# Down products of the two Conv FFN layers: from 24 plain weight tiles per layer to Strassen products over two 256-token halves, in three chunks

## The reference, cut to what matters

```python
def conv_ffn(x, w_up, conv_w, conv_b, w_down):
    u = causal_depthwise_conv(x @ w_up.astype(x.dtype), conv_w, conv_b)
    g, val = jnp.split(u, [FFN_DIM_2], axis=-1)
    return (jax.nn.gelu(g) * val) @ w_down.astype(x.dtype)

def second_block(...):
    ...
        h = h + conv_ffn(rms_norm_2(h, ffn_norm[layer]), ffn_w_up[layer], ffn_conv_w[layer],
                         ffn_conv_b[layer], ffn_w_down[layer])
```

## Time and profile before

| | |
|---|---|
| median of three runs | 2938.49 us |
| lowest, highest | 2938.44, 2938.96 us |
| span of the profiled execution, first to last instruction | 2937.1 us |
| TensorE busy | 2919.6 us, 99% |
| VectorE, ScalarE, GpSimd busy | 1309.0, 1288.6, 1322.3 us |
| up stage of the first layer | about 2000 to 2262 us of the span |
| down stage of the first layer | 2262.57 to 2393.1 us |
| down stage of the second layer | 2802.8 to 2933.5 us |

### The profile page before, as it was taken

The page is one execution under the profiler, slowest core; times in us unless marked ns, Lnnn a source line. Parts: engine busy times, 40 slices in busy tenths (PEclk is TensorE's granted clock), DMA queues, the critical chain, the costliest instruction groups (busy, mean ns, idle before and its releaser), DMA issues.

```text
span 2937.1 us, 40238 instructions
## 1 busy us (share of the span) xinstructions
PE 2919.6 (99%) x14312; PEld 2388.5 (81%) x14312; DVE 1309.0 (45%) x2190; ACT 1288.6 (44%) x2017; POOL 1322.3 (45%) x743
## 2 busy tenths in 40 slices
PE   9999999999999999999999999999999999999999
PEld 7888888888878888888888877778888887888887
DVE  5657534221063667434222076654554138455510
ACT  4556545322253556444223265554444228444421
POOL 4454355444434554455444443444444443444443
PEclk9999999999999999999999999999999999999999
DMA  4222232323322232333333322212333322233333
GB/s 145 73 87 80 81 122 92 99 94 100 108 86 87 73 98 68 94 115 106 94 99 101 108 80 71 61 56 94 98 95 98 95 94 94 93 100 93 100 104 90
DMA packets 77275, 273.37 MB, mean 93 GB/s; under 512 B 8776, under 2 KB 9416, under 8 KB 77152
## 3 DMA queue, kind: packets, MB, share of 16 engines
q1 hardware_dynamic: 74112, 266.05, 29.0%
q10 hardware_dynamic: 3040, 5.64, 0.6%
HBM read 269.55 MB, written 2.10 MB: 92 GB/s over the span
## 4 chain that ended last, share of the span: by engine, by line
PE 93%; DVE 2%; ACT 2%; POOL 1%; issue 1%; DMA 0%; SPq 0%; DVEq 0%; ACTq 0%; POOLq 0%
PE ps L822 25%; PE ps L824 25%; PE ps L823 25%; PE ps L1122 2%; PE ps L1153 2%; PE ps L1100 2%; PE ps L1375 2%; PE ps L1381 1%; PE ps L1376 1%; PE ps L1226 1%; PE ps L1232 1%; PE ps L1227 1%; ACT WHI L1534 1%; PE ps L1095 1%; PE ps L1097 0%
## 5 line engine op out<-in xcount | busy, mean ns | idle before, releaser
L2894 POOL TENSOR_TENSOR WLO<-WRAW,WHI 128x1024 fp32r<-128x1024 f32 x393 | 949.8, 2419 | 1158.5 <-ACT WHI L1534 1158.2
L822 PE MATMUL ps<-HH,WHI 128*128 128x512 f32 x2144 | 842.1, 393 | 2.4 <-POOL WLO L2894 0.9
L824 PE MATMUL ps<-HH,WLO 128*128 128x512 f32 x2144 | 834.8, 389 | 0.0
L823 PE MATMUL ps<-HL,WHI 128*128 128x512 f32 x2144 | 834.4, 389 | 0.0
L1534 ACT ACTIVATE WHI<-WRAW 128x1024 fp32r<-128x1024 f32 x467 | 490.6, 1051 | 281.6 <-DMA WRAW<-wall 280.8
L822 PEld LDWEIGHTS ps<-HH,WHI 128*128 128x128 f32 x2144 | 402.5, 188 | 91.2 <-issue 5.3
L824 PEld LDWEIGHTS ps<-HH,WLO 128*128 128x128 f32 x2144 | 402.4, 188 | 84.7
L823 PEld LDWEIGHTS ps<-HL,WHI 128*128 128x128 f32 x2144 | 402.7, 188 | 81.1
L2746 DVE SCALAR_TENSOR_TENSOR ps<-U,COLS,ps 128x512 f32<-128x512 f32 x192 | 145.0, 755 | 122.6 <-ACT ps L1993 108.5
L2228 DVE TENSOR_TENSOR ACC<-ACC,SQ 128x512 f32<-128x512 f32 x78 | 68.4, 877 | 280.5 <-ACT SQ L1819 271.1
L2980 POOL TENSOR_SCALAR SG<-SG,RS 128x512 f32<-128x512 f32 (+3 forms) x104 | 109.9, 1067 | 141.1 <-DVE RS L2508 141.1
(11 more groups left out here) (422 smaller groups left out, 4805.4 us busy)
## 6 DMA issues: line engine op xcount, KB each, us to landing
WRAW<-wall SPq DMA_DIRECT2D x502, 512.0 KB, 3.5
y<-X ACTq DMA_DIRECT2D x8, 256.0 KB, 4.0
X<-xin SPq DMA_DIRECT2D x3, 512.0 KB, 7.9
DFT<-dft ACTq DMA_DIRECT2D x4, 258.0 KB, 4.3
PT_IN<-pin ACTq DMA_DIRECT2D x2, 512.0 KB, 3.7
DIL<-dil ACTq DMA_DIRECT2D x1, 768.0 KB, 4.6
X<-xin SPq DMA_DIRECT2D x2, 256.0 KB, 4.7
COLS<-cols ACTq DMA_DIRECT2D x1, 290.5 KB, 5.3
```

Of the source, the lines that this page charges most:

```text
L822: pe.matmul(out_, WHI[w_at], x_hi, start=first, stop=False)
L823: pe.matmul(out_, WHI[w_at], x_lo, start=False, stop=False)
L824: return pe.matmul(out_, WLO[w_at], x_hi, start=False, stop=last)
L2894: pool.tensor_tensor(WLO[:, s, :], whole, WHI[:, s, :].bitcast(F32), ALU.subtract).then_inc(wt_lo, 1)
```

## The change

The down stage becomes three chunks. A chunk is 4 rounds of up (8 activation tiles), then a stage `down` that adds these 8 tiles' share to the output. There, output tiles go in pairs, activation tiles in pairs, and tokens in two halves of 256: a 2x2 by 2x2 block product, made by 7 block products instead of 8. Each is three matmuls of 256 columns. The first two chunks have 4 output pairs; the third has 3, and its last two output tiles are made plainly, with two units of 24 matmuls of 512 columns. There are 24 down units per layer as before.

The 7 products need sums. Of the weights: VectorE makes four sums of 128x256 for each paired unit (`sums_of`), one of them in place; ScalarE then splits 1024 and another 768 columns (`split_paired`), and GpSimd the same (`remainder_paired`). Of the activations: VectorE makes three more operations at the end of each up round (`mixed`), ScalarE one copy of 128x1024, VectorE one more remainder of 128x1024. Of the outputs: after each pair, ScalarE copies one half bank out and VectorE makes seven additions (`pair_added`). A pair uses banks 0 to 3 or 4 to 7 in turn. The pairs of a chunk are made one after another, and a pair waits for the additions of the pair two before it. The first pair of a chunk waits until VectorE has emptied all of banks 0 to 3. The loops of `conv_ffn` are written out.

```diff
+CHUNKS = ((0, 4), (4, 4), (8, 4))
...
+PRODUCTS = ((0, "slot", A11, B11), (2, "slot", A12, B21), (4, "slot", A22, T4), (6, "slot", A21, T3),
+            (5, "extra", S1, T1), (1, "extra", S2, T2), (3, "extra", S4, B22))
...
-        if gain:
-            residual("F2", FT2, gain)
+        for k0, m in CHUNKS:
...
+            add("down", 1, pairs * m // 2 + 2 * last, 8, per, made=up, heads=pairs, last=last, gain=gain)
...
+            def down(st):
+                up, blocks = st.made, blocks_of(st)
...
+                for j, (p, b) in enumerate(order_of(st)):
+                    if b == 0 and p == 0:
+                        for k in range(4):
+                            pe.wait_ge(bank_free[st.bank(k)], st.use(k))
+                    if b == 0 and p == 1:
+                        pe.wait_ge(S["product_ready"], up.at("product_ready", 2, up.reps - 1))
+                    if b == 0 and p >= 2:
+                        pe.wait_ge(S["pair_step"], st.at("pair_step", PAIR_STEPS * (p - 1)))
+                    weights(st.unit(j))
...
+                    for i in range(2):
+                        k = 2 * b + i
+                        if p == 0:
+                            pe.wait_ge(S["operand_ready"], up.at("operand_ready", 3, k))
+                        for h, home, block_, x in PRODUCTS:
...
+                            pe.matmul(o, w_hi, FTH[:, row, cols_], start=first, stop=False, skip_group_check=True)
+                            pe.matmul(o, w_hi, FTL[:, row, cols_], start=False, stop=False, skip_group_check=True)
+                            mm = pe.matmul(o, w_lo, FTH[:, row, cols_], start=False, stop=last, skip_group_check=True)
+                    mm.then_inc(unit_used, 1)
...
+            def split_paired(n):
+
+                s, q = n % SLOTS, PAIRED[n]
+                act.wait_ge(raw[s], 16 * (n // SLOTS + 1))
+                act.wait_ge(weights_summed, 4 * q + 2)
+                act.activation(WHI[:, s, :], WRAW[:, s, :], ACT.Copy).then_inc(slot_hi, 1)
+                act.wait_ge(weights_summed, 4 * q + 4)
+                act.activation(XHI[:, q % EXTRA, :], XRAW[:, q % EXTRA, :], ACT.Copy).then_inc(wt_hi, 1)
...
                     for j in range(4):
...
+                        sums_of(st, j, r)
                         dve.wait_ge(unit_used, st.unit(j, r) + 1)
                         scaled(st, j, r, U[:, j, 2:2 + SEQ])
...
+                            if j == 3:
+                                mixed(st, r, halves(SG), (2, 3, 6, 7))
+                            remainder(st, (FTH[:, 4 * r + j // 2, :], FTL[:, 4 * r + j // 2, :]), SG[:, j, :], 1 + j // 2, r)
+                    remainder(st, mixed_rows(r), TM[:, :, :], 3, r)
...
+            def sums_of(st, j, r=0):
...
+                dve.wait_ge(raw[s], 16 * (n // SLOTS + 1))
+                dve.tensor_tensor(sum_of(e, S1), at[A21], at[A22], ALU.add).then_inc(weights_summed, 1)
+                dve.tensor_tensor(at[A21], at[A21], at[A11], ALU.subtract).then_inc(weights_summed, 1)
+                dve.wait_ge(weights_summed, 4 * q + 2)
+                dve.tensor_tensor(sum_of(e, S2), at[A22], at[A21], ALU.add).then_inc(weights_summed, 1)
+                dve.wait_ge(weights_summed, 4 * q + 3)
+                dve.tensor_tensor(sum_of(e, S4), at[A12], sum_of(e, S2), ALU.subtract).then_inc(weights_summed, 1)
...
+            def pair_added(st, p):
...
+                dve.wait_ge(S["first_copied"], st.at("first_copied", p + 1))
+                step(dve.tensor_tensor(t[:, 3, :], t[:, 0, :], bank[0][:, HALF:SEQ], ALU.add))
+                step(dve.tensor_tensor(y1, y1, bank[1][:, :], ALU.add))
+                wait(1)
+                step(dve.tensor_tensor(t[:, 1, :], t[:, 3, :], bank[2][:, HALF:SEQ], ALU.add))
+                step(dve.tensor_tensor(t[:, 2, :], t[:, 3, :], bank[3][:, 0:HALF], ALU.add))
+                step(dve.tensor_tensor(y2, y2, bank[2][:, :], ALU.add))
+                wait(3)
+                step(dve.tensor_tensor(y1, y1, TM[:, 0, :], ALU.add))
+                wait(5)
...
+            def down(st):
+                for j in range(st.units):
+                    p = ended_at(st, j - 1)
+                    if p is not None:
+                        pair_added(st, p)
+                    sums_of(st, j)
...
+            def remainder_paired(n):
...
+                pool.wait_ge(weights_summed, 4 * q + 4)
+                pool.wait_ge(slot_hi, q + 1)
+                pool.tensor_tensor(WLO[:, s, :], WRAW[:, s, :], WHI[:, s, :].bitcast(F32), ALU.subtract)
+                pool.wait_ge(wt_hi, n + 1)
+                pool.tensor_tensor(XLO[:, e, :], XRAW[:, e, :], XHI[:, e, :].bitcast(F32), ALU.subtract).then_inc(wt_lo, 1)
```

More of the change, by code:

```diff
@@ L124, with pair_order @@
 COL, N_COLS = column_plan()
+def pair_order(pairs, blocks):
+    return [(p, b) for p in range(pairs) for b in range(blocks)]
 def unit_list():
@@ L164, in conv_ffn @@
     def conv_ffn(l):
[L165 to L169, removed]
+        for k0, m in CHUNKS:
+            last = 2 * (k0 + m) == FT2
+            for n in range(2 * k0, 2 * (k0 + m)):
+                product("ffn_w_up_2", l, DM, n * P)
+                product("ffn_w_up_2", l, DM, FFN2 + n * P)
+            for p, b in pair_order(DT // 2 - last, m // 2):
+                u.append(("ffn_w_down_2 paired", l, k0 + 2 * b, 2, 2 * p * P, 2 * P))
+            if last:
+                for n in range(DT - 2, DT):
+                    u.append(("ffn_w_down_2", l, 2 * k0 * P, 2 * m * P, n * P, P))
     for c in range(6):
@@ L195 @@
 FOLDS = {n: f for f, n in enumerate(FOLD_UNITS)}
+PAIRED = {n: q for q, n in enumerate(n for n, unit in enumerate(UNITS) if unit[0].endswith(" paired"))}
 HOSTS = ("fourier_branch", "branch_mla")
@@ L540, in build @@
         unit_used = sem("unit_used")
+        weights_summed, slot_hi = sem("weights_summed"), sem("slot_hi")
         bank_free = [sem(f"bank_free{b}") for b in range(BANKS)]
@@ new lines, in down_tail @@
+            def down_tail(st, j0):
+                pe.wait_ge(S["pair_step"], st.at("pair_step", 2 * PAIR_STEPS))
+                for n in range(2):
+                    weights(st.unit(j0 + n))
+                    s, kt = st.unit(j0 + n) % SLOTS, 2 * st.made.reps
+                    for i in range(kt):
+                        row = 4 * (i // 2) + i % 2
+                        mm = three(ps[4 + n][:, :], (slice(None), s, slice(i * P, i * P + P)), FTH[:, row, :], FTL[:, row, :], i == 0, i == kt - 1)
+                    mm.then_inc(unit_used, 1)
@@ new lines, in down @@
+            def down(st):
+                for j in range(st.units):
+                    p = ended_at(st, j - 1)
+                    if p is not None:
+                        pair_added(st, p)
+                    sums_of(st, j)
+                    if st.last and j == st.units - 1:
+                        tail_added(st, DT - 2, j - 1)
+                    p = ended_at(st, j - 2)
+                    if st.last and p is not None:
+                        for t in range(2):
+                            finished(st, 2 * p + t)
+                if st.last:
+                    finished(st, DT - 2)
+                    tail_added(st, DT - 1, st.units - 1)
+                    finished(st, DT - 1)
+                else:
+                    pair_added(st, st.heads - 1)
@@ L2923, in units @@
                 last = st.u0 + st.reps * st.units + AHEAD >= NU
-                repeat(pool, st, body, st.reps if last or st.put_off else 1)
+                repeat(pool, st, body, st.reps if last or st.put_off or st.kind in ("conv_ffn", "down") else 1)
             def operand(st):
```

152 lines of the change are left out of this document (135 added, 17 removed).

## The result

The kernel with the change takes 3026.25 us (median; 3024.66 to 3028.63), the kernel before 2938.47 (2938.44 to 2938.96): 1.0298 times as long, 95% interval 1.0283 to 1.0313. The forecast was 3042 with a range of 2957 to 3085, slower at 0.91. On the span the change costs 3023.6 - 2937.1 = 86.5 us where the sum said 103.4.

What follows compares the result with a forecast made beforehand. TensorE, busy 99% of 2937.1 us, was taken as the bound. Waits of 121.8 us less 18.4 saved gave +103.4, so 3040.5; with 1.4 between span and median, 3042, range 2957 to 3085.

Steps and rivals of the forecast that it cites:

- rows of holding: Earlier trace rows: VectorE operations with two SBUF inputs wait for GpSimd's running one, finishing 0.55 us after (0.29 at 256 columns).
- wait one: At each chunk's start TensorE waits 13.6 us for VectorE to scale tile 3, behind the weight sums.
- wait two: In each chunk's first unit, TensorE waits 2.7 us for the mixed rows of the fourth block row.
- the clock: Low clock after each 13.6 us gap: up to 6 x 1.7 = 10 us, covered by wait two, so none added.
- the lag: The first chunk's opening leaves about 0.7 us more lag in each layer.
- the end of layer one: Last additions and squares come 1 to 2 us later; existing cover just suffices, so nothing; without it 2 us, once.
- the saving: TensorE's matmuls: 119.7 us removed and 110.5 added per layer, saving 9.2 a layer, 18.4 in all.
- nothing either way: Written-out loops neither cost nor save, since the stream shows no hitch at a loop's turn.
- Down, 22.3 in the two layers: Down-stage waits for GpSimd's units and pair additions: 0.45, 1.6, 1.3 and 1.2 us a chunk; third chunk lacks the last two.
- Rival 1: No holding between VectorE and GpSimd: waits 6.2 + 0.4 us a chunk, +21, 2960 us; chance 0.17.
- Rival 2: VectorE's idle shares hide the new work: waits 1.4 us a chunk, -10, 2928 us; chance 0.07.
- Rival 3: Holding chains VectorE and GpSimd in down: 16 us a chunk instead of 4.6, +50, 3092 us; this or beyond, chance 0.16.

Runs made afterwards that it cites:

- run with short GpSimd operations: Changed kernel with GpSimd's two paired subtractions cut to 8 columns and the third product reading the high part again: 2970.83 us.
- the one without sums: Changed kernel with VectorE only signalling in place of each weight sum, ScalarE and GpSimd splitting 768 columns of other data: 2950.85 us.
- bare kernel: Changed kernel with sums, mixed rows, splits, remainders and GpSimd's paired subtractions on 8 columns, TensorE's instructions as many and as wide: 2930.85 us.
- scaling first: Changed kernel with one line moved: in a chunk's last up round VectorE scales its tile before making the four weight sums: 2990.43 us.
- all sums on GpSimd: Changed kernel with the weight sums of the three down units prepared during the last up round made by GpSimd instead of VectorE: 3001.04 us.
- added 512-column matmuls on ones: Changed kernel with extra matmuls keeping TensorE busy in the gap at each chunk's start: 3138.21 us with 40, 3025.94 with 12.

## Why the prediction was right, and where its sum was off

**The direction and the mechanism** were right. The bound was read from VectorE's timeline and not from its 53% share of the up stage, and the rows of holding were read as a rule for every operation with two SBUF inputs. Both carried it; the run with short GpSimd operations and the one without sums show each by itself.

**The size.** The forecast of 3042 was 16 us above the measured 3026, and that is smaller than the errors in it: wait one, wait two with the clock, the down stage and the lag were some 26 us too high together, the end of layer one and the saving some 10 us off the other way.

**Saved 18.4.** Nearly right: 17.3, at 0.1202 us a matmul in the bare kernel instead of 0.1196.

**Wait one, 13.6.** Right in place and cause, too large by 2.2: 11.37 beyond the pitch, 68.2 instead of 81.6. Tile 0 of the last round is scaled 3.3 late, not 4.4, and tile 3 about 10.2, not 12.6. The chain was built with the looped hand-offs of the earlier trace rows, and "nothing either way" for the written-out loops was wrong for VectorE's queue. Four tap waits at 0.26 and two remainder waits at 0.23 would be 1.5 us in one round, an estimate from the two kernels' rows. Four sums also take 1.62 us to the next start (short GpSimd run), not 1.8. How the 2.4 divides between these and where the sums fell against GpSimd, no run separates.

**Wait two, 2.7, and the clock, 0.** In the changed kernel wait two is 0.3 us once, and about 12 us go at the low clock in the first units, 1.4 to 2.8 a chunk, where the earlier trace rows had 1.7. As terms both are wrong; their sum, forecast at 16.2, is 12.3. The text's "covered by wait two" was the correct relation, but it held the other way round: the low clock is seen, and wait two is what it hides.

**Down, 22.3 in the two layers.** Smaller: 14.6, with 9.2 of waits for GpSimd and 1.7 for pair additions. The lag of 0.7 from a first chunk's opening (1.4 in all) did not come: the start waits 11.2 in every chunk.

**End of layer one, 0.** Wrong by 8.9. The tail waits 4.3 us for `pair_added` of pair 1, and then loses 1.5 at the low clock. That addition is queued behind the squares of pair 0, which GpSimd's subtractions of the tail's units hold:

```profile
2415.87 2.88 DVE L2383 SCALAR_TENSOR_TENSOR HL<-X,COLS,HH 128x512 fp32r<-128x512 f32 x1
2418.67 2.88 DVE L2374 TENSOR_TENSOR ACC<-ACC,SQ 128x512 f32<-128x512 f32 x1
2421.48 0.41 DVE L2959 TENSOR_TENSOR TM<-TM,ps 128x256 f32<-128x256 f32 x1
```

The prediction asked only when the last square comes and not what the first ones stand in front of. The other 3.0 is the norm, whose sum found its cover gone, as the text said it could ("2 us, once"): 1.4 of waiting and 1.6 at the low clock behind it.

**Rivals.** Rival 1 (2960, no holding) is what the run with short GpSimd operations comes near: 2971, with the sums' own time still ahead of the scaling and 12.5 us at the low clock. Rival 2 (2928, VectorE's idle shares hide all) is about the bare kernel, 2930.9, for which all added work has to go. Even the least start cost, 1.25 a chunk, is 40% of the 3.1 at which the change breaks even. Rival 3 (the closed chain through the whole down stage) did not come: the waits for GpSimd stay at or under 1.3.

**No version beats the kernel before.** The best with all its work in it are the three with scaling first in the strict order, 2989.5 to 2990.4, 1.7 to 1.8% slower than before. They differ in which wait comes last and not in time. Between 2086 and 2134 VectorE is busy 42.6 of 48 us in the changed kernel, the holding included; these orders only move what stands in that queue. That no other order could win was not shown.

## What to carry to other kernels

A saving in the bounding engine's work is worth what is left after the turn between stages: price the helpers' work at the moment it is due, by walking their queue from the last slack on, and count any two-input VectorE operation beside GpSimd at GpSimd's remaining time. In a queue, work that someone waits for goes ahead of work due later; one moved line was worth 36 us here, twice the 18 us that the change was after. When one wait is moved, look for the operand behind it that is late by as much; and before a pair or tile order is changed, count which units covered the additions that free its banks.

## What the runs showed of the hardware that was not expected

- A semaphore hand-off from ScalarE to VectorE in a written-out stage is about 0.25 us shorter than in a loop (0.85 against 1.11, 0.70 against 0.93), with no effect on the time while nobody waits for VectorE.
- In the first gap of 11.2 us the granted clock is 1.00 in the first two stretches of 2 us, 0.87 in the third and 0.50 after; the first unit of renewed full work takes 6.4 to 7.8 us instead of 5.04. The 1.1 us waits of the bare kernel leave the clock at 1.00. With scaling first, the 3.2 us wait at the start left it at 1.00 in two of the six chunks and was followed by 0.50 in four (a first unit of 5.1 us against 6.6 to 7.6).
- The holding between VectorE and GpSimd goes both ways: beside VectorE's mixed rows, one of GpSimd's sums of 256 columns took 1.19 us, not 0.74 (all sums on GpSimd).
- The added 512-column matmuls on ones, with both operands plain f32 and not fp32r, took 0.845 us each, 3.7 times the 0.2267 of the earlier trace rows. Which of the two differences, type or broadcast operand, does it was not separated.
